# Latent attention in one run of 64 tiles, with queries, keys and scores in rounded parts and rests

## What is computed

```
c_q, c_kv, k_pe = split(h @ w_in, [768, 1024])           # 768, 256, 32 columns
q  = (rms_norm(c_q) @ w_uq).reshape(l, 16, 64 + 32)      # q_nope, q_pe
kv = (rms_norm(c_kv) @ w_ukv).reshape(l, 16, 64 + 64)    # k_nope, v
# rope on q_pe and on k_pe of the latent tokens; one k_pe is shared by all 16 heads
s  = einsum('bqhd,bkhd->bhqk', q, k) * 96 ** -0.5        # 512 queries, 768 keys
o  = softmax(s) @ v ;  out = o @ w_out
```

## Time and profile before

| | us |
|---|---|
| median of three runs | 2552.12 (2552.01 to 2563.15) |
| span of the profiled execution | 2557.3 |
| PE busy | 2422.4 (95%) |
| DVE, ACT, POOL busy | 1164.6, 705.2, 157.7 |
| from the first query projection to the output projection | 1791.1 to 2125.6 |

### The profile page before, as it was taken

How to read it: one execution, slowest core, us unless ns; L and a number is a source line. 1 busy time by engine, 2 the same in 40 slices (tenths; PEclk the granted TensorE clock), 3 DMA queues, 4 the chain that set the end, 5 groups by cost and what they waited for, 6 DMA issues and landing times.

```text
span 2557.3 us, 30384 instructions
## 1 busy us (share of the span) xinstructions
PE 2422.4 (95%) x12638; PEld 1731.6 (68%) x12638; DVE 1164.6 (46%) x1976; ACT 705.2 (28%) x1243; POOL 157.7 (6%) x157
## 2 busy tenths in 40 slices
PE   8998999999999998899999999999989989899998
PEld 6783563333445987648888888877756557788886
DVE  3247432111464768643443342443374584544444
ACT  2235012111133344324112112123253362322222
POOL 0000011111104015100000000000000000000000
PEclk9999999999999999999999999999999999999999
DMA  9937659898401211312122112102100101332222
GB/s 344 360 131 264 240 202 378 328 362 311 160 21 35 67 50 50 132 33 79 54 66 67 66 59 67 57 33 90 56 13 1 66 1 33 107 95 92 92 91 76
DMA packets 181032, 308.84 MB, mean 121 GB/s; under 512 B 18459, under 2 KB 90003, under 8 KB 180768
## 3 DMA queue, kind: packets, MB, share of 16 engines
q1 hardware_dynamic: 167792, 278.40, 31.3%
q0 software_dynamic: 12368, 26.35, 3.0%
q10 hardware_dynamic: 736, 2.15, 0.2%
HBM read 355.05 MB, written 18.93 MB: 146 GB/s over the span
## 4 chain that ended last, share of the span: by engine, by line
PE 61%; DVE 9%; ACT 3%; issue 2%; DMA 0%; DVEq 0%; ACTq 0%; POOL 0%
PE PS L136 38%; PE PS L2536 11%; PE PS L148 3%; PE PS L2474 2%; PE PS L142 2%; PE PS L2953 2%; DVE X L106 2%; DVE sm L117 1%; PE PS L2480 1%; DVE H L106 1%; PE PS L2412 1%; DVE rest L106 1%; DVE gate L106 1%; DVE MIX L106 1%; DVE H L114 1%
## 5 line engine op out<-in xcount | busy, mean ns | idle before, releaser
L136 PE MATMUL PS<-at,wH 128*128 128x512 f32 (+1 forms) x2144 | 563.3, 352 | 3.7 <-DVE at L106 3.7
L136 PEld LDWEIGHTS PS<-at,wH 128*128 128x128 f32 x2144 | 378.2, 189 | 58.5 <-DVE at L106 2.6
L136 PE MATMUL PS<-at,rest 128*128 128x512 f32 (+1 forms) x1072 | 376.4, 351 | 0.0
L2536 PE MATMUL PS<-wH,ac 128*128 128x512 f32 x880 | 277.9, 393 | 3.3 <-DVE hn L106 3.3
L106 DVE TENSOR_TENSOR rest<-ring,wH 128x2048 fp32r<-128x2048 f32 x66 | 150.3, 2290 | 211.2 <-ACT wH L129 210.6
L136 PEld LDWEIGHTS PS<-at,rest 128*128 128x128 f32 x1072 | 202.7, 189 | 27.3
L129 ACT CAST wH<-ring 128x2048 fp32r<-128x2048 f32 x66 | 124.7, 1907 | 264.7 <-PE PS L2536 199.8
L2536 PEld LDWEIGHTS PS<-wH,ac 128*128 128x128 f32 x880 | 165.2, 188 | 43.2 <-DVE hn L106 8.4
L2536 PE MATMUL PS<-rest,ac 128*128 128x512 f32 x440 | 171.5, 390 | 0.0
L136 PE MATMUL PS<-HI,ATr 128*128 128x256 f32 x512 | 148.1, 289 | 4.2 <-DVE MIXr L106 3.8
L136 PE MATMUL PS<-ring,AT 128*128 128x512 f32 x320 | 141.7, 599 | 0.8 <-ACT AT L129 0.8
(11 more groups left out here) (369 smaller groups left out, 3981.7 us busy)
## 6 DMA issues: line engine op xcount, KB each, us to landing
R<-in_w_gate_up_dram SPq DMA_DIRECT2D x32, 1024.0 KB, 14.0
ring<-in_w_down_dram SPq DMA_DIRECT2D x32, 1024.0 KB, 13.2
ring<-in_w_gate_up_dram SPq DMA_DIRECT2D x32, 1024.0 KB
ring<-in_w_ffn_gate_dram SPq DMA_DIRECT2D x22, 1024.0 KB, 5.5
ring<-in_w_ffn_up_dram SPq DMA_DIRECT2D x22, 1024.0 KB, 5.4
ring<-in_w_ffn_down_dram SPq DMA_DIRECT2D x22, 1024.0 KB, 4.9
ring<-in_w_ada_dram SPq DMA_DIRECT2D x16, 1024.0 KB, 7.4
HIw<-in_w_gate_up_dram SPq DMA_DIRECT2D x16, 1024.0 KB, 8.7
```

Source lines behind the costliest of these rows:

```text
L136: ins = self.e.matmul(out, l, r, start=k == 0, stop=k == len(pairs) - 1)
L2536: ins = p.e.matmul(bk(4 + n_dn % 3), a_, b_, start=start and i == 0, stop=stop and i == len(terms) - 1)
```

## The change

**Queries and keys come out turned.** Projections now have the weights as the stationary operand, two heads (a pair g, 0 to 7) wide, and the tokens as the moving one: `q_nope_pe` is 18 rounded matmuls 128x512, `k_nope_pe` 6 of 128x512 and 6 of 128x256. The result needs no transposes. Only the rope part of the queries is still made with tokens on the partitions (`q_pe_pe`, 18 rounded 128x256 for a token tile and half), roped, and turned pair by pair (`q_pe_turn`, four transposes); k_pe is turned once. v has its own product (`v_pe`, 6 rounded 128x512 for a token tile and half).

**Parts and rests.** c_q and c_kv get a rounded part (ACT) and a rest (DVE) within `latent_*`. The weights get theirs from ACT (`pe_high`, `wq_high`, `kn_high`, `v_high`) and POOL (`*_low`). Queries and keys of each pair are copied out of PSUM as rounded part by ACT and as rest by DVE (`q_split`, `k_split`, `q_pe_split`, two instructions of each engine in each). A score tile is `three` of 128x512 and `three` of 128x256. The scale 96 ** -0.5 is put into the norm weights of c_q.

**One run of 64 tiles.** Only pair 0 is made ahead. All else is dealt between tiles by tables that give the tile at which a piece stands. Before each piece PE waits in `taken` until ACT and DVE have taken every earlier piece out of PSUM. The second half's weights are split at tiles 19 to 27.

**POOL** takes over the rests of the output weights and of the head outputs from DVE, and loads the two gate rows later, after v.

```diff
-        for n in range(35):
-            if n < 32:
-                h, t = units2[n]
...
-                p.each([(bk(b), qTm[:, h, 128 * t:128 * t + 128], kTm[:, h, 0:512]),
-                        (bk(b + 1, 256), qTm[:, h, 128 * t:128 * t + 128], kTm[:, h, 512:768])], inc=S("score2"))
...
+    V_AT = {0: 0, 1: 1, 2: 2, 35: 3, 36: 4, 37: 5}
+    QP_AT = {23: 0, 24: 1}
+    QN_AT = {4: 1, 9: 2, 16: 3, 28: 4, 32: 5, 41: 6, 49: 7}
+    KN_AT = {3: 1, 11: 2, 17: 3, 27: 4, 33: 5, 43: 6, 51: 7}
+    PT_AT = {5: 1, 13: 2, 19: 3, 29: 4, 39: 5, 45: 6, 53: 7}
+    WP_AT, WQ_AT = {19: 0, 20: 1, 21: 2}, {22: 0, 23: 1, 24: 2}
+    OH_AT = {51: (0, 1), 53: (2, 3), 58: (4,), 59: (5,), 60: (6,), 66: (7,)}
+    WO_AT = {54: 0, 55: 0, 56: 1, 57: 1, 61: 2, 62: 2, 63: 3, 64: 3}
...
+    def taken(p):
+        p.wait_ge(S("v_take"), count(p, "v_m"))
+        p.wait_ge(S("q_pe_copy"), count(p, "q_pe"))
+        for x, y in (("q", "q_nope"), ("k", "k_nope"), ("q_pe", "q_pe_T")):
+            p.wait_ge(S(x + "_high"), 2 * count(p, y))
+            p.wait_ge(S(x + "_low"), 2 * count(p, y))
...
+    def q_nope_pe(p, g):
+        hf, x = g // 4, 2 * (g % 4)
+        p.wait_ge(S("wq_low"), 3 * hf + 3)
+        p.wait_ge(S("cq_low"), 8)
+        ws = [(nqH[k // 2][:, 8 * (k % 2) + x:8 * (k % 2) + x + 2, :], nqL[hf][k // 2][:, 8 * (k % 2) + x:8 * (k % 2) + x + 2, :])
+              for k in range(6)]
+        p.acc(bk(7), three(ws, [(cqH(k), cqL[:, k, :]) for k in range(6)]), inc=S("q_nope"))
...
+                qs = [(q2(g, e, 0)[ALL[e], ts_], q2(g, e, 1)[ALL[e], ts_])]
+                for t0, ln in ((0, 512), (512, 256)):
+                    p.acc(PS[:, 512 * b + t0:512 * b + t0 + ln],
+                          three(qs, [(k2(g, e, 0)[ALL[e], t0:t0 + ln], k2(g, e, 1)[ALL[e], t0:t0 + ln])]),
+                          inc=S("score2") if t0 else None)
...
+            if n in QN_AT:
+                taken(p)
+                q_nope_pe(p, QN_AT[n])
```

More of the change, by code:

```diff
@@ L277, in program, with piece @@
     U = []
[L279 to L280 removed]
+    def piece(src, freed, hi=None, pool=False):
+        U.append(dict(src=src, k=src.shape[0] // P, n=src.shape[1], freed=freed, hi=hi, hi_free=None, ord=None, pool=pool))
     def pieces512(w, freed):
@@ new lines, in kn_high, with kn_low, v_high @@
+    def kn_high(a, hf):
+        landed(a, UQ[hf] + 3)
+        a.wait_ge(S("k_nope"), 4 * hf)
+        a.cast(nkH, kvF[hf][:, :, 0:64], inc=S("kv_high"))
+    def kn_low(g, hf):
+        g.wait_ge(S("kv_high"), 3 * hf + 1)
+        g.wait_ge(S("wq_low"), 3 * hf + 3)
+        for k in range(2):
+            g.tt(nkL[hf][k], kvF[hf][:, 8 * k:8 * k + 8, 0:64], nkH[:, 8 * k:8 * k + 8, :].bitcast(F32), ALU.subtract, inc=S("kv_low"))
+    def v_high(a, hf):
+        a.wait_ge(S("q_pe"), 4 * hf + 4)
+        for k in range(2):
+            a.cast(vH[k], kvF[hf][:, 8 * k:8 * k + 8, 64:128], inc=S("kv_high"))
@@ new lines, in q_pe_pe @@
+    def q_pe_pe(p, hf, t):
+        p.wait_ge(S("pe_low"), 3 * hf + 3)
+        p.wait_ge(S("cq_low"), 2 * t + 2)
+        ts_ = slice(128 * t, 128 * t + 128)
+        p.acc(bk(QB[hf][t], 256), three([(cqH(k)[:, ts_], cqL[:, k, ts_]) for k in range(6)],
+                                        [(peH[k // 2][:, 8 * (k % 2):8 * (k % 2) + 8, :], peL[hf][k // 2][:, 8 * (k % 2):8 * (k % 2) + 8, :])
+                                         for k in range(6)]), inc=S("q_pe"))
+    def q_nope_pe(p, g):
[5 more added lines that the diff above has]
+        p.acc(bk(7), three(ws, [(cqH(k), cqL[:, k, :]) for k in range(6)]), inc=S("q_nope"))
@@ new lines, in k_nope_pe @@
+    def k_nope_pe(p, g):
+        hf, x = g // 4, 2 * (g % 4)
+        p.wait_ge(S("kv_low"), 4 * hf + 2)
+        p.wait_ge(S("ck_low"), 6)
+        ws = [(nkH[:, 8 * k + x:8 * k + x + 2, :], nkL[hf][k][:, x:x + 2, :]) for k in range(2)]
+        for t0, ln, o_ in (((0, 256, 3328), (256, 512, 3584)) if g else ((0, 512, 1024), (512, 256, 1536))):
+            p.acc(PS[:, o_:o_ + ln], three(ws, [(ckH[:, k, t0:t0 + ln], ckL[:, k, t0:t0 + ln]) for k in range(2)]),
+                  inc=S("k_nope") if t0 else None)
@@ new lines, in q_pe_turn, with v_pe @@
+    def q_pe_turn(p, g):
+        p.wait_ge(S("q_rope"), 4 * (g // 4) + 4)
+        x, b = 64 * (g % 4), 7 if g else 6
+        p.turns([(PS[0:96, 512 * b + 128 * t:512 * b + 128 * t + 128], qx[t][:, x:x + 96]) for t in range(4)], ident, S("q_pe_T"))
+    def v_pe(p, m):
+        hf, t = m // 6, m % 6
+        p.wait_ge(S("kv_low"), 4 * hf + 4)
+        p.wait_ge(S("ck_low"), 6)
+        ts_ = slice(128 * t, 128 * t + 128)
+        p.acc(bk(7 - m % 2), three([(ckH[:, k, ts_], ckL[:, k, ts_]) for k in range(2)],
+                                   [(vH[k], kvL[hf][:, 8 * k:8 * k + 8, 64:128]) for k in range(2)]), inc=S("v_m"))
@@ new lines, in heads_act @@
+            if n == 3:
+                a.settle()
+                for e in range(2):
+                    a.cast(k2(1, e, 0)[PE_[e], :], k2(0, e, 0)[PE_[e], :].bitcast(F32), inc=S("k_pe_high"))
+            if n in WP_AT:
+                pe_high(a, 1, WP_AT[n])
+            if n in WQ_AT:
+                wq_high(a, 1, WQ_AT[n])
+            if n == 25:
+                kn_high(a, 1)
+            if n == 27:
+                v_high(a, 1)
+            if n in OH_AT:
+                a.wait_ge(S("q_nope"), 8)
+                a.wait_ge(S("k_nope"), 8)
+                a.settle()
+                for k in OH_AT[n]:
+                    a.cast(oH(k), oT[:, k, :], inc=S("o_high"))
```

519 lines of the change are left out of this document (326 added, 193 removed).

## The result

The changed kernel takes 2537.95 us (median of 4 runs, 2534.73 to 2540.59) against 2554.4 beside it (4 runs): a ratio of 0.9927, 95% interval 0.9905 to 0.9949. A second set of five runs, beside 13 of the kernel before (2554.49), gave 2540.47, ratio 0.9935 (0.9915 to 0.9956). So it saves 14 to 17 us where 40 were forecast: faster, as predicted, but by under half the size, and just outside the range.

The account below looks back on a forecast made before the run. PE was taken to bound the rewritten stretch: 252.3 us of its work plus 42 of waits make 294.3 against 334.6, 40 less. So 2552.1 - 40 = 2512 us, range 2490 to 2536.

Parts of the forecast that it names:

- The price list: PE's work in the rewritten stretch, priced per matmul and transpose: 302.9 us before, 252.3 after, 50.6 less.
- (a): Start of the query projections: waits for the third piece of weights to land and be split, about 2 us later.
- (b): Before tile 0: PE waits 5 us for copies and rests, plus 2 us for the clock after such a wait.
- step (d): Run of tiles: 3.1 us of waits in eight tiles, times eight, 25 us; bounds 11 and 58.
- step (e): POOL slows DVE's product, showing in the last tiles: 4 us; bounds 0 and 26, or 34 with a whole-operation lock.
- POOL holds DVE: Rival: in the run of tiles POOL's operations cost 26 us in place of 4, time 2534; chance 0.10.
- The clock rival: Waits at every piece bring PE to half clock for part of the run; at half its work, 2630 us; chance 0.03.
- PE leads in all five stages: Rewritten stretch before the change: PE is busiest in every stage; less PE work pays fully only while DVE stays under it.
- The sign set for a run over 285: Tile run over 285 us: waits under-counted, and the chain should name rests of queries and keys ahead of PE.
- near 266: Expected length in us of the tile run, from first scores to the output projection.
- The signs also named DVE: In the profile after, PE would wait on DVE, for maximum and product, more than on ACT.

Follow-up runs that it names:

- rope_fill: Changed kernel with rope pieces one tile later, weights split before them, and useless matmuls before tile 0 and in the last tiles: 2529.78 us, 0.9903 of the kernel before.
- two_terms: Changed kernel without the scores' term with the rest of the keys (128 rounded matmuls less): 2535.72 us, 0.9916 of the kernel before.
- four_terms: Changed kernel with a fourth score term, rest times rest (128 rounded matmuls more): 2545.29 us, 0.9959 of the kernel before.

## Why the prediction was right and wrong

**Right.** The price list: PE's work in the stretch 50.3 less for 50.6, at full clock. The start, (a): 45.9 against 44.0; POOL's rest of the third piece ends at 1786.54, 0.1 before the first query product. Before tile 0, (b): 22.8 for 23, with the six rests in the chain. The rests' durations. The direction.

**Wrong: step (d), the run of tiles.** It took eight tiles that hold one pair, found 3.1 us of waits by hand, and multiplied by eight. In the tiles that it followed the count was good: work of 27.3 and 3.1 make 30.4, and from the maximum of tile 8 to that of tile 16 it was 29.5. For tiles 40 to 53, made of such pairs, that gives 48.0 + 5.5 = 53.5, and 55.7 came (the lesser of the two executions, as all below). But the tiles are not all alike. Work and 0.39 per tile, and measured:

| tiles | forecast | measured |
|---|---|---|
| 0 to 5 | 26.8 | 30.8 |
| 6 to 15 | 37.7 | 34.6 |
| 16 to 22 | 28.1 | 33.1 |
| 23 to 29 | 34.0 | 43.7 |
| 30 to 39 | 45.9 | 47.8 |
| 40 to 53 | 53.5 | 55.7 |
| 54 to 62 (with POOL's 4) | 32.8 | 27.7 |

The sum over all is 14.7 more. Tiles 23 to 29 are 9.7 over and 16 to 22 5.0; the other five groups cancel (4.0, 1.9 and 2.2 over, 3.1 and 5.1 under). The two hold what a standard pair does not: the second half's rope and weights, and two pieces in neighbouring tiles. Freeing the rope took some 6 back from the one. Of the 5.0 in the other up to 2.3 are the clock, and the rest is not explained. What the first six tiles lose 4 to, beside the dips, was not tried.

**Wrong in place: step (e), POOL.** It looked for the hold in the last tiles and at the product, though the row that gave the price is itself an operation on `R` and `con`, the rope's form. There it costs nothing that shows, and the takeover even pays about 1. It also took 1.0 for the longest hold, from operations of 512; the second half's weights have operations of 1024, which take 2.39. The rival "POOL holds DVE" took in the whole run, at 26; what is shown is some 6, in two tiles. In the Trainium skill, "SBUF — State Buffer", section "Who interferes with whom", it says that any DVE instruction with two inputs in SBUF contends with a GpSimd instruction that reads SBUF, and that a reduction on this chip never does. The rows agree: the rope's product of `R` and `con` went from 0.76 to 2.80 for two, the rest of `PS` and `Rr`, with one input in SBUF, kept 0.686 (three of them beside POOL at 0.68), and the maximum 0.953 (twelve beside POOL, 0.94 to 0.96), though it reads PSUM here, so no row tests a reduction of SBUF. Had the rule been applied to each DVE form beside POOL, the rope would have been on the list.

**Mis-sized: the clock in step (b).** It stood for 2 us at one place. Eight dips came in place of two. They cost at most the 15.4 us that their work would save. Behind tile 0's scores it is 1.3 in tile 0 (2.3 from scores to maximum in place of 1.04), 4.7 in the intervals, and 1.6 at the end (11.95 in place of 10.4 in `rope_fill`). That is 7.6 of the missing 22.8, and a lower bound: the 12.7 us of work in dips that both executions had can hold up to 6.3 more. So the clock has 8 to 14 of the 22.8 and the waits 9 to 15, of which the held ropes are some 6; the other 3 to 9 no run took apart. Where the same tiles can be seen with dips and without, as 0 to 5, 6 to 15 and 30 to 39 in the changed kernel (30.8, 36.0, 49.8) and in `rope_fill` (29.9, 35.0, 47.8), 9.7 us of work at half speed cost 3.9. The clock rival was right in kind at a tenth of its price. The prediction set it aside because two rows of eight tiles stood at 1.00; they said nothing of the other 48. The rule named there, in the Trainium skill, "TensorE: Matmul & The Clock Gate", section "A second HAM failure mode: psum-queue depth-cycling" (short idle times between groups of matmuls make the clock swing), agrees with the eight dips better than it did with the rows of before.

**The reason behind the steps.** "PE leads in all five stages, so less of its work pays" was taken as full price. With PE at 27.3 us a pair and DVE at 22.8 the lead was real but the pieces stand in order on three engines. The sign set for a run over 285 came true: from first scores it is 292.4 ("near 266" is a slip beside the sum's own terms, which make 236 + 25 + 4 + 4 = 269). In the chain of the run DVE's rests of queries and keys have 5.0%, behind its maxima with 6.3% and ACT's copies of probabilities with 5.9%. The signs also named DVE as the one that PE would wait for; of PE's 43.5 us without work in the run, 28.2 ended with ACT (its copies of probabilities above all) and 7.7 with DVE. `two_terms` and `four_terms` put the price of PE's work at a fifth. What exactly the loop is that sets a plain tile (maximum, exponential, product, transposes, copies over two pairs of banks) no run took apart, and it stays open.

## What to carry to other kernels

Before pricing a cut in the busiest engine's work, ask what its price will be after the cut: an engine at 85% in a chain of tiles is not the bound in each tile, and one run that adds the same amount of useless work tells the slope. Do not multiply a hand count of one group of tiles by their number; list the tiles that carry something else (a second half's weights, a rope) and count those. When work goes to GpSimd, list the VectorE operations with all operands in SBUF that will run at the same time (here rope and product), and put the one on the path elsewhere. Before two profiles are compared group by group, look where the clock was at half in each.

## What the runs showed of the hardware

- TensorE's granted clock fell to half eight times in one execution of the changed kernel and nine times in another, at places that moved in part, while 50 of 63 tile intervals stayed equal to 0.1 us. With 32 useless matmuls 11.7 us less work stood at half clock (19.7 for 31.4).
- A VectorE operation with all operands in SBUF that started behind GpSimd's ended 0.4 to 0.6 after it: 2.18 for 0.62, and 2.80 for 0.76 (a pair), beside operations of 2.39.
- A VectorE rest with one operand in PSUM keeps its price beside GpSimd (0.686 for 0.683).
